# One set of sums in place of two: the split-precision product as three 256-column matmuls

## The reference

```python
h = rmsnorm(x, norm_g[l]) * (1.0 + scale[:, None]) + shift[:, None]
q, k, v, up, uf, g = split_proj(h @ w_in[l])
...
xn = rms_norm(x, norm_mix[layer])
h = xn @ even_w_in[i]
...
x = x + mix
x = x + memory_cross_attention(...)
def squared_relu_mlp(xn, w_up, w_down):
    return jnp.square(jax.nn.relu(xn @ w_up)) @ w_down
x = x + squared_relu_mlp(rms_norm(x, norm_ffn[layer]), ffn_up[layer], ffn_down[layer])
```

## Time and profile before

| | us |
|---|---|
| median of 3 runs | 3987.93 (3987.42 to 3990.09) |
| the profiled execution's own time | 3990.47 |
| its span, first to last instruction | 3989.1 |
| PE busy | 3781.2 (95%) |
| PEld busy | 3214.8 (81%) |
| DVE busy | 2581.6 (65%) |
| ACT busy | 1796.3 (45%) |
| POOL busy | 1481.1 (37%) |

### The profile page before, as it was taken

One profiled execution on the slowest core, in us unless ns is written; L12 is line 12 of the kernel. 1 busy time (PEld: TensorE's weight loads), 2 busy tenths in 40 slices (PEclk: granted clock), 3 DMA queues, 4 the chain that ended last, 5 costly groups with the idle time before them and its releaser, 6 DMA issues.

```text
span 3989.1 us, 64444 instructions
## 1 busy us (share of the span) xinstructions
PE 3781.2 (95%) x27348; PEld 3214.8 (81%) x27348; DVE 2581.6 (65%) x3660; ACT 1796.3 (45%) x2793; POOL 1481.1 (37%) x726
## 2 busy tenths in 40 slices
PE   6898999998998999989999999999989989999998
PEld 3687888787877887888778888888878878888887
DVE  0435644785368897668879676876666875445457
ACT  1435343654355444445544443444445553333334
POOL 0332343233322441004344444444644434444443
PEclk8999999999999999999999999999889999999999
DMA  9663665354543443005345565556445435454553
GB/s 387 267 234 148 246 248 232 128 193 183 227 190 108 182 181 113 23 24 217 145 172 222 197 243 190 222 227 257 153 175 195 175 139 193 174 192 183 190 190 127
DMA packets 60848, 746.92 MB, mean 187 GB/s; under 512 B 7040, under 2 KB 9216, under 8 KB 17168
## 3 DMA queue, kind: packets, MB, share of 16 engines
q1 hardware_dynamic: 49536, 696.74, 46.0%
q0 software_dynamic: 8960, 43.95, 2.9%
q10 hardware_dynamic: 2064, 2.10, 0.1%
HBM read 725.92 MB, written 16.84 MB: 186 GB/s over the span
## 4 chain that ended last, share of the span: by engine, by line
PE 78%; DVE 13%; ACT 5%; DMA 2%; issue 1%; POOL 1%; another core or an unknown queue 0%; SPq 0%; DVEq 0%; ACTq 0%; POOLq 0%
PE ps L369 44%; PE ps L370 22%; DVE pieces L322 2%; DMA ring<-in_ada 2%; PE ps L2260 2%; ACT pieces L306 2%; PE ps L790 2%; PE ps L3626 1%; DVE r L1204 1%; DVE opa L570 1%; PE ps L1930 1%; DVE scr L591 1%; PE ps L643 1%; ACT scr L674 0%; ACT opa L886 0%
## 5 line engine op out<-in xcount | busy, mean ns | idle before, releaser
L369 PE MATMUL ps<-opa,pieces 128*128 128x512 f32 x6192 | 2243.9, 405 | 54.0 <-DVE pieces L322 36.1
L340 POOL TENSOR_TENSOR pieces<-ring,pieces 128x1024 fp32r<-128x1024 f32 x539 | 1341.1, 2488 | 2167.6 <-ACT pieces L306 2153.3
L370 PE MATMUL ps<-opa,pieces 128*128 128x256 f32 x6192 | 1739.2, 281 | 0.0
L306 ACT ACTIVATE pieces<-ring 128x1024 fp32r<-128x1024 f32 (+1 forms) x1110 | 1098.5, 1036 | 818.9 <-PE ps L370 818.1
L369 PEld LDWEIGHTS ps<-opa,pieces 128*128 128x128 f32 x6192 | 1169.1, 189 | 353.0 <-issue 32.6
L370 PEld LDWEIGHTS ps<-opa,pieces 128*128 128x128 f32 x6192 | 1175.2, 190 | 7.7 <-issue 5.3
L369 PE MATMUL ps<-opb,pieces 128*128 128x512 f32 x2560 | 909.2, 396 | 18.7 <-DVE pieces L322 13.0
L322 DVE TENSOR_TENSOR pieces<-ring,pieces 128x1024 fp32r<-128x1024 f32 (+1 forms) x571 | 720.2, 1261 | 265.8 <-ACT pieces L306 262.6
L370 PE MATMUL ps<-opb,pieces 128*128 128x256 f32 x2560 | 725.4, 283 | 0.0
L369 PEld LDWEIGHTS ps<-opb,pieces 128*128 128x128 f32 x2560 | 482.8, 189 | 140.7 <-issue 15.5
L370 PEld LDWEIGHTS ps<-opb,pieces 128*128 128x128 f32 x2560 | 483.3, 189 | 0.1
(11 more groups left out here) (435 smaller groups left out, 3321.4 us busy)
## 6 DMA issues: line engine op xcount, KB each, us to landing
ring<-in_up SPq DMA_DIRECT2D x64, 2048.0 KB, 7.7
ring<-in_down SPq DMA_DIRECT2D x64, 2048.0 KB, 7.8
ring<-in_win SPq DMA_DIRECT2D x56, 2048.0 KB, 7.6
ring<-in_ada SPq DMA_DIRECT2D x48, 2048.0 KB, 11.9
ring<-in_wout SPq DMA_DIRECT2D x24, 2048.0 KB, 7.5
ring<-in_evin SPq DMA_DIRECT2D x18, 2048.0 KB, 7.9
ring<-in_evout SPq DMA_DIRECT2D x8, 2048.0 KB, 7.9
ring<-in_xkv SPq DMA_DIRECT2D x8, 2048.0 KB, 7.7
```

The source lines that it names most:

```text
L306: a.do.activation(K.parts_of(p)[0][:, s, :], w[:, s, :], ACT.Copy).then_inc(*K.hi.up((p, h)))
L340: g.do.tensor_tensor(lo[:, s, :], w[:, s, :], hi[:, s, :].bitcast(F), ALU.subtract).then_inc(*K.lo2.up(p))
L369: pe.do.matmul(b[:, 0:512], hi[:, k, :], op[:, 512 * k:512 * k + 512], start=i == 0, stop=False)
L370: t = pe.do.matmul(b[:, 0:256], lo[:, k, :], half(op, 0, k), start=False, stop=i == kt - 1)
```

## The change

A step of k becomes three matmuls of 256 columns, all onto the first 256 words of the bank: `lo` by high, `hi` by high, `hi` by low. Nothing is written to the second half, so the evictions no longer add. `dve_sum` is a copy. `dve_normed` and its variant are one multiplication that reads PSUM. `dve_onto` and `dve_wout` do one addition per tile. The bank is freed by the multiplication, where the reduction freed it (`evn` for `evs`, and so on).

```diff
     for i, k in enumerate(order):
         pe.wait_ge(*(K.lo2 if k >= 8 else K.lo).of(p))
         pe.wait_ge(*K.dve.of((*opkey, k)))
-        pe.do.matmul(b[:, 0:512], hi[:, k, :], op[:, 512 * k:512 * k + 512], start=i == 0, stop=False)
-        t = pe.do.matmul(b[:, 0:256], lo[:, k, :], half(op, 0, k), start=False, stop=i == kt - 1)
+        pe.do.matmul(b[:, 0:256], lo[:, k, :], half(op, 0, k), start=i == 0, stop=False)
+        for z in range(2):
+            t = pe.do.matmul(b[:, 0:256], hi[:, k, :], half(op, z, k), start=False, stop=i + z == kt)
...
 def dve_sum(K, p, out):
     m = out.shape[0]
-    b = K.bank["tile", p][0:m, 0:512].rearrange("p (z t) -> p t z", z=2)
     K.v.wait_ge(*K.tile.of(p))
-    return K.v.do.tensor_reduce(out, b, AX.X, ALU.add)
+    return K.v.do.tensor_copy(out, K.bank["tile", p][0:m, 0:256])
...
-def dve_normed_by_fours(K, p, out, rstd, key):
-    v, o = K.v, by_fours(out)
-    v.wait_ge(*K.tile.of(p))
-    v.do.tensor_reduce(o, K.bank["tile", p][:, 0:512].rearrange("p (z k r) -> p k r z", z=2, r=4), AX.X,
-                       ALU.add).then_inc(*K.dve.up(key))
-    v.wait_ge(*K.dve.of(key))
-    return v.do.tensor_tensor(o, o, in_fours(rstd), ALU.mult)
+def dve_normed_by_fours(K, p, out, rstd):
+    K.v.wait_ge(*K.tile.of(p))
+    return K.v.do.tensor_tensor(by_fours(out), in_fours(K.bank["tile", p][:, 0:256]), in_fours(rstd), ALU.mult)
...
 def dve_onto(K, p, x, key):
     v, b = K.v, K.bank["tile", p]
     v.wait_ge(*K.tile.of(p))
-    v.do.tensor_tensor(x, b[:, 0:256], x, ALU.add).then_inc(*K.dve.up())
-    v.wait_ge(*K.dve.now())
-    v.do.tensor_tensor(x, b[:, 256:512], x, ALU.add).then_inc(*K.dve.up(key))
+    v.do.tensor_tensor(x, b[:, 0:256], x, ALU.add).then_inc(*K.dve.up(key))
...
-def dve_normed(K, p, out, rstd, key):
+def dve_normed(K, p, out, rstd):
     v = K.v
-    dve_sum(K, p, out).then_inc(*K.dve.up(key))
-    v.wait_ge(*K.dve.of(key))
-    return v.do.tensor_tensor(out, out, rstd[0:out.shape[0]], ALU.mult)
+    m = out.shape[0]
+    v.wait_ge(*K.tile.of(p))
+    return v.do.tensor_tensor(out, K.bank["tile", p][0:m, 0:256], rstd[0:m], ALU.mult)
...
         v.wait_ge(*K.tile.of(p + n))
-        for z in range(2):
-            v.do.scalar_tensor_tensor(out=x, in0=b[:, 256 * z:256 * z + 256], scalar=K.ada[l][:, 32 + n, s:s + 1], in1=x,
-                                      op0=ALU.mult, op1=ALU.add).then_inc(*K.dve.up(("x", l, s, n)))
-            if z == 0:
-                v.wait_ge(*K.dve.now())
+        v.do.scalar_tensor_tensor(out=x, in0=b[:, 0:256], scalar=K.ada[l][:, 32 + n, s:s + 1], in1=x,
+                                  op0=ALU.mult, op1=ALU.add).then_inc(*K.dve.up(("x", l, s, n)))
```

More of the change, by code:

```diff
@@ L1683, in pe_evin @@
         side = None if n else pe_totals(K, ("nf",), ("nm", 0))
-        pe_tile(K, K.first["evin"] + n, K.opa, ("nm", 0, "h"), (K.dve, ("evs", n)), side, 6)
+        pe_tile(K, K.first["evin"] + n, K.opa, ("nm", 0, "h"), (K.dve, ("evn", n)), side, 6)
         pe_dsa_ahead(K, n)
@@ L1755, in dve_evin @@
                 v.wait_ge(*K.dve.of(("ev", n - 2)))
-        dve_normed(K, p + n, d, K.rr, ("evs", n)).then_inc(*K.dve.up(("evn", n)))
+        dve_normed(K, p + n, d, K.rr).then_inc(*K.dve.up(("evn", n)))
 MAG = 12582912.0
@@ L2892, in pe_xattn @@
         side = None if n else pe_totals(K, ("nx", l), ("nmem", l))
-        pe_tile(K, p + n, K.opb, ("nx", l, "h"), (K.dve, ("xq", l, n)), side, 6)
+        pe_tile(K, p + n, K.opb, ("nx", l, "h"), (K.dve, ("xqn", l, n)), side, 6)
     p = K.first["xkv", l]
@@ L2898, in pe_xattn @@
         side = pe_xvturn(K, l, n - 5) if n > 4 else None
-        pe_tile(K, p + n, K.opa, ("nmem", l, "h"), (K.dve, ("xkv", l, n)), side, 5)
+        pe_tile(K, p + n, K.opa, ("nmem", l, "h"), (K.dve, ("xkvn", l, n)), side, 5)
         if n > 4:
@@ L2987, in dve_xattn @@
             dve_scaled(K, K.opa, ("nmem", l, "h"), k, K.mem[:, k, :], nm(k))
-        dve_normed(K, p + n, K.QX[:, n, :], K.rstd, ("xq", l, n)).then_inc(*K.dve.up(("xqn", l, n)))
+        dve_normed(K, p + n, K.QX[:, n, :], K.rstd).then_inc(*K.dve.up(("xqn", l, n)))
     p = K.first["xkv", l]
@@ L2992, in dve_xattn @@
         dve_feed(K, ahead(K, p + n))
-        dve_normed(K, p + n, K.KX[:, n, :] if n < 4 else K.yb[n - 4], K.rmem, ("xkv", l, n)).then_inc(*K.dve.up(("xkvn", l, n)))
+        dve_normed(K, p + n, K.KX[:, n, :] if n < 4 else K.yb[n - 4], K.rmem).then_inc(*K.dve.up(("xkvn", l, n)))
         for _ in range(1 + (n > 0)):
@@ L3101, in dve_ffn @@
                 v.wait_ge(*K.dve.now())
-            dve_normed(K, p + n, h, K.rstd, ("usum", l, q, n)).then_inc(*K.dve.up())
+            dve_normed(K, p + n, h, K.rstd).then_inc(*K.dve.up(("usum", l, q, n)))
             v.wait_ge(*K.dve.now())
@@ L3472, in pe_odin @@
         side = None if n else pe_totals(K, ("nm", 1))
-        pe_tile(K, K.first["odin"] + n, K.opa, ("nm", 1, "h"), (K.dve, ("us", n)), side, 6)
+        pe_tile(K, K.first["odin"] + n, K.opa, ("nm", 1, "h"), (K.dve, ("u", n)), side, 6)
         if n in ORDER_K:
@@ L3527, in dve_odin @@
             v.wait_ge(*K.dve.now())
-        dve_normed_by_fours(K, p + n, K.U[:, n, :], K.rstd, ("us", n)).then_inc(*K.dve.up(("u", n)))
+        dve_normed_by_fours(K, p + n, K.U[:, n, :], K.rstd).then_inc(*K.dve.up(("u", n)))
         for _ in range(min(n - 12, 2)):
```

## The result

The changed kernel takes 4007.6 us (median of 4 runs, 4005.7 to 4013.1) where the kernel before, run beside it, took 3988.5 (4 runs, 3987.4 to 3990.1). The ratio is 1.005, with an interval from 1.0032 to 1.0067: it is slower by 19 us. Timed again on another chip (the last experiment) the ratio was 1.0055. The forecast of 3972 had the wrong sign; 4007.6 lies inside the range, between the times of the second rival (3988) and the first (4043).

A forecast was written before the change was run, and what follows sets the result against it. PE was taken to set the time, nearly by columns streamed, with DVE mattering only where PE waits. From the 3987.9 us median, +4 for PE and -20 for relief gave 3972 us; the 8-in-10 range was 3905 to 4055.

The forecast's parts named there:

- PE's term: Main-product steps: three 256-column matmuls replace 512 plus 256 columns; mean +0.5 ns a step, times 8752, +4 us.
- stand in just that position: Each new matmul was priced like line 370's 256-column one, followed by other weights: 118.6 ns at 3550 us, 116.7 at 3850.
- The bound of +8.6 ns: Upper bound for a main-product step: 256-column matmuls settling at 0.12 us give 360 against 351.4 ns, +75 us.
- The load at nothing: The 8752 added weight loads, 0.19 us each in the record, were costed at nothing beyond the step, covered by streaming.
- The 113 ns of the earlier trace: Shortest spacing seen between full 128x128 loads; as the step's lower bound 339 against about 352 ns, -114 us.
- DVE's saving: Lighter evictions save DVE up to 378 of 2581.6 us, most under PE's work; copy and PSUM multiplication put at 0.42.
- The relief: PE's waits shortened by lighter DVE: a third of 62 us, -20 us; bounds 0 and -46.
- The four waits: PE's waits for low pieces (33 us after the start), attention outputs (12.3), operand parts (10.0) and line 381 (7.0): 62 us.
- Rival 1: Slower, 4043 us: a matmul costs PE more than its columns, +8.6 ns a step; decides above 2.3 ns; chance 0.27.
- Rival 2: No difference, 3988 us: DVE was hidden anyway, and PE's waits also end in chains through ACT and POOL; chance 0.20.
- Rival 3: Much faster, 3854 us: main-product steps close up to the loads' spacing, -114 us; chance 0.08.
- Rival 4: Weight loads become the bound: three of 0.19 without overlap, 570 ns per step, +1908 us, 5876 us; chance 0.02.

The follow-up runs named there:

- the last experiment: The changed kernel, unedited, timed again in five rounds on another chip against the kernel before: 4010.6 us against 3990.0, ratio 1.0055.
- the cuts: Kernel before, with the 512-column matmul in the MLPs cut into 256+256, 320+192, 384+128 or 448+64, all but each tile's first step: 4139.5 us in one run.
- the eviction-alone kernel: The changed kernel with the two matmuls of before, evictions reading the first half only, hi by low left out: 3944.7 us, ratio 0.9884 to before.
- the matmuls alone: Kernel before, with hi's 512 columns split into two 256-column matmuls after each tile's first step, eviction unchanged: 4046.0 us against 3990.8, ratio 1.014.
- the kernel with the normed tiles alone: Kernel before, but `dve_normed` reads only the bank's first half in one multiplication, hi by low left out there: 3965.2 us against 3990.0, ratio 0.9941.
- the halves: The change's two parts run separately against the kernel before: more matmuls with the old eviction, +55 us; light eviction with the old matmuls, -46 us.

## Why the prediction was wrong

**The step that failed is PE's term:** "The mean is +0.5 ns, 8752 x 0.5 = +4 us". It measured +7.5 ns in the steps that were free in both traces, 8752 x 7.5 = +66 us. (By other ways: the means of the cuts 2 x 119.3 - 233.2 = 5.4, without the third matmul; PE's busy time against before 5.6, where before's holds standing time that no list shows (see the relief), and against the eviction-alone kernel 6.4; the matmuls alone 6.7; the two medians 7.7.) In its own terms, the premise failed that the three new matmuls "stand in just that position" and so cost what line 370's cost between two of 512 columns. In `opa` the reading was right (116.7; 116.6 in the mean), but among their own kind the same matmuls took 119.9: 350.0 forecast, 359.8 measured. In `opb` the forecast of 355.8 met the measured 356.1 by luck: over seven steps, from starts rounded to 10 ns, line 370 was read as 118.6 where its mean is 120.5, and three of those would be 361.5. The forecast then took the mean of a loss and a gain (+4.4 at 3550 us in `opb`, -3.3 at 3850 in `opa`) as if the places weighed the same, where 6192 steps of 8752 read `opa`. Two readings that differ by more than their mean do not fix a sign, and 2.3 ns were enough to turn it. The bound of +8.6 ns held in the mean.

A page of the Trainium skill had a price for it that I did not use: "TensorE: Matmul & The Clock Gate", section "Back-to-back issue gap", adds a constant of 2.5 ns to each matmul at 2.4 GHz. The page gives this for matmuls by themselves and says that in a stream with weight loads the loads set the spacing too. Worked out from it, as an estimate, one more start per step is 8752 x 2.5 = +22 us. The traces show 7.5 ns, and they decide; the sign was the page's.

**The load at nothing** failed with it. What a load costs is not its record of 0.19 us, which overlaps others, but a few ns of a matmul: a step of three went from 342 to 360 ns in one product and from 350 to 356 in the other when the loads went from 64 to 128 columns, 2 to 6 ns for each. The 113 ns of the earlier trace rows were not a pace for matmuls that stream 256 columns.

**DVE's saving** was right: 336 us against "up to 378", with 0.424 and 0.424 as forecast.

**The relief** was mis-sized: -20 against -46. The four waits that I took a third of did fall by 23 us. What the list left out is time of PE that it does not show as waiting. In the kernel before, in PE's timeline near 2596 us:

```profile
2595.85 0.28 PE L370 MATMUL ps<-opa,pieces 128*128 128x256 f32 x1
2596.68 0.47 PE L369 MATMUL ps<-opa,pieces 128*128 128x512 f32 x1 [0.55 <-DVE pieces L322]
```

From start to start it is 0.83 us, where 0.12 is the rule: 0.71 late. The list says 0.55, since it counts from the modelled end. With 0.16 for each of the 41 waits for low pieces that the eviction-alone kernel no longer has, 6.6 us stay hidden, and its PE is indeed busy for 6.7 us less with the same matmuls. (That the two meet so closely is one case: the kernel with the normed tiles alone has 13 waits fewer, and 11.5 us less.) The account of its profiled execution is: 6.7, and 207.9 - (3957.3 - 3774.5) = 25.1 of standing still, make the 31.8 by which the span is shorter. That execution took 3958.6, 14 us above the median of its kernel; where those 14 lie is open.

**The balance** of the two profiled executions is +49.0 - 31.8 = +17 us, or by steps +61.1 - 40.4 = +20.7 in the main products and -3.5 in the rest. From the halves, each measured by itself, it is 6.7 x 8752 = +59 and -46, or +13; with the free steps' 7.5 it is +66 and -46, or +20; measured were +19 and +21, forecast +4 - 20 = -16. **Rival 1** came, with its mechanism and its point of decision (2.3 ns); its 4043 was too high because it kept the relief at 20 (26 us) and took 8.6 ns for 7.5 (10 us). **Rival 2** falls with the eviction-alone kernel, 3988 forecast and 3944.7 measured. **Rival 3** falls: the free steps took 356 to 360 ns in the mean, not 339. **Rival 4** falls: PEld is busy for all of the window, and the step grew by some 7 ns, not by 218.

Not settled: whether the fixed part belongs to the load's columns or to the outputs written; why the pace of a row of matmuls, and what a cut costs there, goes with the operand buffer; and how much of the 6 to 11 us between the halves and the whole is waiting that the slower matmuls hid, since the intervals do not separate it.

## What to carry to other kernels

Where an edit has a multiplier of thousands, price it from counts over whole stages (matmuls in windows of 100 us), and take it from several places: if they differ by more than the term, find out whether that is error or a property of the place (here the operand buffer), and weigh the places by their counts; until then the sign is unknown, and the term belongs into the range, not into the forecast. What an instruction costs beside a neighbour of another kind need not be what it costs among its own. A longer instruction stream on the engine that sets the time is paid in every tile, a relief of another engine only in the tiles where that engine was late: make the change in those tiles alone, which here turned +0.5% into -0.6%. And a list of waits understates what a late engine costs where ends are modelled; compare the distances between starts.

## What the runs showed of the hardware

At a granted clock of 1.00, a matmul with a full 128-column load took 0.445 ns per column and some 5 ns besides, and in the cut steps full loads followed one another no closer than 108 ns; a matmul of 64 to 192 columns and the one of 256 behind it took 228 to 230 ns together. Among its own kind a matmul of 256 columns took 119.9 ns in tiles that read one operand buffer and 118.7 in those that read the other; between two of 512 columns it took 116.6 and 120.5. With a load of 64 or 32 columns it took 114 to 117 ns, with 64 rows and 128 columns 119 to 120. A multiplication of 256 columns on DVE took 0.424 us with one input in PSUM and 0.908 in the mean with both in SBUF.
